# One-hot tiles of a gate-spreading stage hold four tokens side by side in place of eight

## The reference

```python
q = (xt @ w_query).reshape(t, PEER_HEADS, 2, PEER_KEY_DIM // 2)
sc = jnp.einsum('thpd,hpnd->thpn', q, sub_keys)        # 8 heads, 2 halves, 128 keys
s1, i1 = lax.top_k(sc[:, :, 0], 16); s2, i2 = lax.top_k(sc[:, :, 1], 16)
top_s, ci = lax.top_k(cand, 16)                        # cand = all sums s1 + s2
experts = i1[ci // 16] * 128 + i2[ci % 16]             # one of 128 x 128
gate = softmax(top_s)
act = gelu(einsum('thkd,td->thk', u_tab[experts], x))
y = einsum('thk,thkd->td', gate * act, v_tab[experts])
```

## Time and profile before

| | us |
|---|---|
| median of 3 runs | 3759.57 |
| lowest, highest run | 3704.11, 3778.11 |
| span of the profiled execution | 3695.5 |

### The profile page before, as it was taken

The page is one execution under the profiler, slowest core; times in us unless marked ns, Lnnn a source line. Parts: engine busy times, 40 slices in busy tenths (PEclk is TensorE's granted clock), DMA queues, the critical chain, the costliest instruction groups (busy, mean ns, idle before and its releaser), DMA issues. The chain is left out here.

```text
span 3695.5 us, 47408 instructions
## 1 busy us (share of the span) xinstructions
PE 3222.9 (87%) x15880; PEld 1722.0 (47%) x15880; DVE 2426.2 (66%) x4231; ACT 1106.9 (30%) x1480; POOL 1984.6 (54%) x1490
## 2 busy tenths in 40 slices
PE   7957789899999999999999999688887877878887
PEld 3423754455555555555555556333333333333333
DVE  2693964115676875555555553488899868788887
ACT  4312353223444443343433433211111111111112
POOL 1353550112444344323232327689988886988886
PEclk8978888999999998989999999798998998989999
DMA  3200011112333334554455447788888886888886
GB/s 107 69 0 23 0 46 74 46 45 77 105 115 112 107 119 144 189 186 177 166 183 192 177 165 263 259 274 294 303 279 277 288 298 227 287 278 277 286 266 239
DMA packets 260396, 648.61 MB, mean 176 GB/s; under 512 B 16992, under 2 KB 115552, under 8 KB 257136
## 3 DMA queue, kind: packets, MB, share of 16 engines
q1 hardware_dynamic: 186176, 378.33, 29.7%
q0 software_dynamic: 74160, 269.52, 21.2%
HBM read 542.39 MB, written 105.91 MB: 175 GB/s over the span
## 5 line engine op out<-in xcount | busy, mean ns | idle before, releaser
L91 POOL TENSOR_TENSOR w_low<-w_ring,w_high 128x1024 f16<-128x1024 f32 x164 | 471.7, 2877 | 1316.5 <-ACT w_ring L86 1316.4
L1640 PE MATMUL psum<-vh,wh 128*128 128x512 bf16 x1536 | 608.1, 396 | 283.0 <-POOL wl L1689 255.9
L1227 PE MATMUL psum<-region_y,w_high 128*128 128x384 f16 x2048 | 703.8, 344 | 18.3 <-POOL w_low L91 16.6
L1228 PE MATMUL psum<-region_y,w_high 128*128 128x384 f16 x2048 | 702.7, 343 | 0.0
L1229 PE MATMUL psum<-region_y,w_low 128*128 128x384 f16 x2048 | 701.3, 342 | 0.0
L1641 PE MATMUL psum<-vl,wh 128*128 128x512 bf16 x1536 | 606.5, 395 | 0.0
L1642 PE MATMUL psum<-vh,wl 128*128 128x512 bf16 x1536 | 603.8, 393 | 0.0
L1656 ACT ACTIVATE vh<-w_ring 128x1024 bf16<-128x1024 f32 x128 | 134.8, 1053 | 1051.5 <-DMA w_ring<-in_v_t_dram 1029.9
L1640 PEld LDWEIGHTS psum<-vh,wh 128*128 128x128 bf16 x1536 | 155.2, 101 | 491.0 <-issue 310.3
L1260 PE MATMUL psum<-scores 128*128 128x128 bf16 x1536 | 373.9, 412 | 4.5 <-DVE scores L1469 4.5
L1685 POOL TENSOR_TENSOR vl<-w_ring,vh 128x1024 bf16<-128x1024 f32 x128 | 341.7, 2670 | 21.7 <-ACT vh L1656 21.1
(11 more groups left out here) (227 smaller groups left out, 5326.1 us busy)
## 6 DMA issues: line engine op xcount, KB each, us to landing
w_ring<-in_u_t_dram SPq DMA_DIRECT2D x128, 512.0 KB, 3.7
w_ring<-in_v_t_dram SPq DMA_DIRECT2D x128, 512.0 KB, 5.3
acts_dram<-ge SPq DMA_DIRECT2D x128, 384.0 KB, 2.5
gates_dram<-scores SPq DMA_DIRECT2D x24, 2048.0 KB, 7.3
gt<-gates_dram SPq DMA_DIRECT2D x32, 1536.0 KB, 9.5
at<-acts_dram SPq DMA_DIRECT2D x32, 1536.0 KB, 13.0
w_ring<-in_w_stream_dram SPq DMA_DIRECT2D x20, 512.0 KB, 3.3
w_ring<-in_w_q_dram SPq DMA_DIRECT2D x16, 512.0 KB, 3.2
```

The costliest lines, as they stand in the source:

```text
L91: pool.tensor_tensor(self.wl[:, s, :], self.wf[:, s, :], self.wh[:, s, :], ALU.subtract).then_inc(self.w_lo, 1)
L1227: pe.matmul(a, uh[:, par, row], xh[:, n, cols], start=(n == 0), stop=False)
L1228: pe.matmul(a, uh[:, par, row], xl[:, n, cols], start=False, stop=False)
L1640: pe.matmul(a, wh[:, par, c, rows], vh[:, par, c, cols], start=(c == 0), stop=False)
```

## The change

`hot`, the octet's tiles, goes from (i, t) with t of 8 to (q, i, t) with q of 2 and t of 4. The octet is still of eight tokens, each tile has still 1024 elements and is written by one instruction, but it holds two halves one after the other, in each of which four tokens lie side by side for every key value i. The matmuls read their operands at a step of four elements in place of eight. DVE's operands get one dimension more: the picks and gates of four tokens are repeated 128 times in each half, and the comparison reads a new table `iota_4` (128 times 4 elements, repeated for both halves), which one added copy makes out of `iota_x` ahead of the first octet.

```diff
+    QUAD = OCT // 2
...
-        "p (r n i t) -> p r n i t", r=2, n=4, i=P)
+        "p (r n q i t) -> p r n q i t", r=2, n=4, q=2, i=P)
...
+    at += P * OCT // 2
+    iota_4 = flat[:, at:at + P * QUAD // 2].bitcast(BF16).rearrange("p (q i t) -> p q i t", q=1, t=QUAD)
...
                 for b in range(2):
-                    for q in range(4):
-                        t = 4 * b + q
+                    for t in range(QUAD):
                         for part in (2, 3):
-                            last = pe.matmul(psum[:, 4 + 2 * r + b, q * P:(q + 1) * P], hot[:, r, 0, :, t],
-                                             hot[:, r, part, :, t], start=(part == 2), stop=(part == 3))
+                            last = pe.matmul(psum[:, 4 + 2 * r + b, t * P:(t + 1) * P], hot[:, r, 0, b, :, t],
+                                             hot[:, r, part, b, :, t], start=(part == 2), stop=(part == 3))
...
                 def per_token(ap):
-                    return ap.rearrange("p (a t) -> p a t", a=1).to_broadcast([P, P, OCT])
+                    return ap.rearrange("p (q a t) -> p q a t", q=2, a=1).to_broadcast([P, 2, P, QUAD])
+
+                iota = iota_4.to_broadcast([P, 2, P, QUAD])
...
-                dve.tensor_tensor(hot[:, r, 1, :, :], iota_x, per_token(picks[:, 1, tokens]),
-                                  ALU.is_equal).then_inc(two_hot, 1)
-                dve.tensor_tensor(hot[:, r, 0, :, :], iota_x, per_token(picks[:, 0, tokens]), ALU.is_equal)
+                dve.tensor_tensor(hot[:, r, 1], iota, per_token(picks[:, 1, tokens]), ALU.is_equal).then_inc(two_hot, 1)
+                dve.tensor_tensor(hot[:, r, 0], iota, per_token(picks[:, 0, tokens]), ALU.is_equal)
...
             dve.wait_ge(iota_in, 32)
+            dve.tensor_copy(iota_4.rearrange("p q i t -> p (q i) t"), iota_x[:, :, 0:QUAD])
             dve.tensor_copy(parts[:, 0, :], gate[:, :]).then_inc(pre, 1)
```

## The result

| | before | after |
|---|---|---|
| median | 3734.15 us (4 runs, 3704.11 to 3778.11) | 3459.41 us (4 runs, 3441.17 to 3469.28) |
| ratio | | 0.933, 95% interval 0.9305 to 0.9354 |
| span of the profiled execution | 3695.5 us | 3458.6 us |

Two of the four runs of the kernel before, 3760 and 3778, lie well above the other two, and the ratio leaves the slowest of them out: it is 3459.4 over 3708.7, the median of the other three. On another occasion seven runs of the kernel before were all between 3694.2 and 3710.7 with the median at 3701.0, and the changed kernel beside them took 3445.9 (4 runs), a ratio of 0.9304 (0.9284 to 0.9324). So the change saves 249 to 255 us, not the 275 between the medians of the table.

The account below looks back on a forecast made before the run. PE was taken to bound the octets' stage; 48 slots shortened from 16.85 to 11.04 us save 279 us, so 3760 - 279 = 3481 us. The range was 3400 to 3570, the forecast's own 3440 to 3525.

Parts of the forecast that it names:

- What bounds the stage: Octets' stage: PE sets the pace and stays the bound by little; DVE is next, with 9.23 us a slot.
- 86 were forecast: Octets' stage: DVE's waiting for PE falls from 352 us to 48 × 1.8 = 86 or so.
- a slot of 11.04: Octets' stage: a new slot of two half slots of 5.52 us takes 11.04 us, against 16.85 before.
- The step as the price: Octet matmuls: the moving operand's step of eight bf16 costs 1.8 ns an element, hence 0.232 us a matmul.
- I take 0.100: Octet matmuls at a step of four: 0.100 us each, likeliest 0.085 to 0.120, against 0.232 before.
- the full rate: Rival, octet matmuls: 0.054 to 0.081 us each, slot 9.57 to 10.43, time 3411 to 3452 us; chance 0.22.
- The loss: PE's low clock after octets: its 1.59 us a slot was taken to vanish with the shorter octets.
- the sum said 279: Octets' stage: 5.81 us saved a slot, 4.22 in octet matmuls and 1.59 in the clock, times 48 is 279 us.
- the price of 0: DVE's four octet instructions: inner runs of four cost nothing more, argued from line 621's short runs.
- The added copy: Ahead of the first octet: the copy of 512 elements costs 0.5 us once, up to 2 if POOL holds it up.
- 276 forecast: Octets' stage: DMA's mean grows from 181 to 276 GB/s with the shorter slot.
- The tight handover: SP's queue: the `u_t` load after a `gates` store has 10.1 us to land; it can cost a few tenths.

Follow-up runs that it names:

- the run with doubled octets: The changed kernel with each octet's 16 matmuls issued twice over the same PSUM: 3618.10 us.
- two side by side: The changed kernel with two tokens side by side in place of four, so TensorE reads at a step of 2 elements: 3421.18 us.
- the run with thin stores: The version with two tokens side by side, each store of the gates' tile moving a quarter of its 2 MB: 3362.26 us.

## Why the prediction was right

- **What bounds the stage** was read rightly: PE, before and after. PE is busy without a break in both. DVE waits for it 79.9 us where 86 were forecast, but that the two agree is luck: 86 goes with a slot of 11.04, and at the 11.6 measured the same sum (11.6 - 9.23, 48 times) gives 114. DVE's waits for PE and for gathered rows, 79.9 + 47.4, are 127.
- **The step as the price.** Right, and shown: the moving operand alone brings the time back. The 16-byte lines of the Trainium skill's page "SBUF — State Buffer" (section "Door 1: The DMA port swizzle") fit these runs, in which the distance grows up to a step of 16 bytes and not beyond (0.232 and 0.234), but neither of its figures holds: at two elements in each line the rate was half (0.117 against 0.056), and at a step of 8 bf16 a quarter. Four bf16 in a line were enough (0.058).
- **Its size was off.** The term that was mis-sized is "I take 0.100": it measured 0.117, within the forecast's 0.085 to 0.120. The working had the right value beside it, 0.116, from 1.8 ns for every further 16 bytes shared by two elements. It was drawn down by the thought that 0.09 was near, as the weight load lasts 98 ns. That thought was false: pairs ran at 0.056 with weight loads of 97 and 98 ns, and at 0.119 with one of 146. For the same reason the chance of the full rate was argued against with the wrong row, and line 1031's 0.11 says nothing of these pairs: its operands are f32, and bf16 pairs of 128 contiguous columns come at 0.056. The Trainium skill's page "TensorE: Matmul & The Clock Gate" (section "Back-to-back issue gap") gives 81 ns for such pairs when sustained, and that was too high as well.
- **The clock.** The loss vanished as assumed: 70 to 74 us by the run with doubled octets, 76 in the sum (48 × 1.59). Why it would was left open, and two runs narrow it: neither long octets alone nor wide distances alone bring it.
- **The slot** is 11.6 us where 11.04 was forecast, the stage gave 250 us where the sum said 279. Of the difference 32 matmuls × 0.017 × 48 = 26 us are the one term.
- **DVE.** Its four instructions stayed at 0.68 to 0.69, so the price of 0 was right, but line 621 was no evidence for it. From its f32 instructions, 0.41 us for 256 elements, to the 1.22 us of line 1493 for 1024 it is (1.22 - 0.41) / 768 = 1.05 ns an element; by this estimate they went one element at a time anyway and had no rate of two to lose. The bf16 instructions, 0.69 us for 1024 elements, had it, and lost it at runs of one (1.22 us). The added copy took 0.294 us once (0.5 forecast).
- **DMA.** 260 GB/s for 276 forecast, by the longer slot. The tight handover that was named, the load of `u_t`, didn't show here (with two side by side ACT waited 24.4 us for it); what came late were the gathered rows, 47 us of waiting in DVE's spare time.
- **The median.** 3481 against 3459 (and 3446 the second time) looks closer than the sum was: the two medians of the kernel before, 3760 at the forecast and 3701 later, moved by more than the error of the sum. 3701 - 279 would have been 3422, 24 below what that comparison gave.

## What to carry to other kernels

Compare the distance between the starts of two matmuls with their columns: where 128 columns take clearly more than a third of what 384 take, look at the step of the moving operand, and lay tiles out so that at least four bf16 of each 16 bytes are read (0.058 against 0.117 with two of them); the stationary operand matters far less (0.002 here). The engine that writes the tile sets the other end: DVE kept its rate at inner runs of two (0.68 us), and lost it at one (1.22). And when PE gets faster, work out the transfers per slot beforehand: here a slot moves 2.9 MB (half a `gates` store, a load of `u_t`, a store of `acts`, 1 MB of gathered rows), which in the 9.64 us of two side by side would be some 300 GB/s, and the rows came late at 280.

## What the runs showed of the hardware that was not expected

- The step at which reads slow down: at 4 bytes nothing (0.058 against 0.056), at 8 bytes twice, at 16 and at 32 bytes four times the floor. One price of 1.8 ns for each further 16 bytes fits all five, if it is hidden where four or more elements share them.
- A weight load's duration grows by less (98, 117, 146 ns), and the matmuls don't keep its pace, even where it is longer than the distance between them (146 ns against 0.119 us).
- With PE always busy, the clock fell only where octets were both long (3.7 us) and sparse (0.23 a matmul). With one of the two, 1.00 was granted in the window from 1500 to 1900 us. It also fell after pauses of PE, to 0.50.
- A bf16 instruction of DVE of 0.68 us took 2.6 where it met POOL's line 91, and ended 0.55 us after it, 39 times in the run with thin stores.
